# Rotary stage of a hybrid attention and state-space block: how the key norms are formed, and in what order four engines work

## The reference

```python
def rms_norm(u, g):
    uf = u.astype(F32)
    return (uf * lax.rsqrt(jnp.mean(uf * uf, -1, keepdims=True) + RMS_EPS) * g).astype(u.dtype)

def apply_axial_rope(u, cos, sin):
    ...
    out = jnp.stack([u1 * cs - u2 * sn, u1 * sn + u2 * cs], axis=-2)

out_a = window_sink_attention(apply_axial_rope(to_heads(aq), cos, sin), apply_axial_rope(to_heads(ak), cos, sin), ...)
cbk, cbv = rms_norm(to_heads(cbk), k_gain), to_heads(cbv)
out_b = global_block_attention(apply_axial_rope(rms_norm(to_heads(bq), q_gain), cos, sin),
                               apply_axial_rope(rms_norm(to_heads(bk), k_gain), cos, sin), ...)
```

## Time and profile before

| | us |
|---|---|
| median of three runs (lowest, highest) | 3442.82 (3438.43, 3443.50) |
| the profiled execution, its own time | 3442.47 |
| its span from first to last instruction | 3440.7 |
| the stage in layer 0, first instruction to attend's first product | 168.05 to 211.55 |
| the stage in layer 1 | 1999.22 to 2037.95 |

### The profile page before, as it was taken

How to read it: one execution, slowest core, us unless ns; L and a number is a source line. 1 busy time by engine, 2 the same in 40 slices (tenths; PEclk the granted TensorE clock), 3 DMA queues, 4 the chain that set the end, 5 groups by cost and what they waited for, 6 DMA issues and landing times. The chain is left out here.

```text
span 3440.7 us, 44530 instructions
## 1 busy us (share of the span) xinstructions
PE 3234.4 (94%) x17014; PEld 2739.6 (80%) x17014; DVE 1777.7 (52%) x2884; ACT 1009.9 (29%) x1949; POOL 1382.1 (40%) x1027
## 2 busy tenths in 40 slices
PE   5979989899999999999998979989899999999997
PEld 4768878788788888888886759878787788888886
DVE  8377958685673333333235867936776511311224
ACT  5257742361430000000003347732453300000003
POOL 0154213264444344343444354212354444454454
PEclk9979999999999999999999979999999999999999
DMA  8200023003111212111111610011022111111111
GB/s 332 74 1 1 1 101 107 21 25 123 59 52 62 67 67 68 66 61 61 43 37 66 228 38 1 1 50 50 13 86 80 49 55 49 43 55 49 43 55 50
DMA packets 69808, 214.12 MB, mean 62 GB/s; under 512 B 6816, under 2 KB 19104, under 8 KB 68256
## 3 DMA queue, kind: packets, MB, share of 16 engines
q1 hardware_dynamic: 62224, 183.86, 15.5%
q10 hardware_dynamic: 7440, 28.34, 2.3%
HBM read 192.78 MB, written 19.40 MB: 62 GB/s over the span
## 5 line engine op out<-in xcount | busy, mean ns | idle before, releaser
L205 PE MATMUL ps<-h_hi,f_whi 128*128 128x512 f32 (+1 forms) x1760 | 650.2, 369 | 3.5 <-DVE f_gated L3379 3.5
L206 PE MATMUL ps<-h_lo,f_whi 128*128 128x512 f32 (+1 forms) x1760 | 648.6, 369 | 0.0
L207 PE MATMUL ps<-h_hi,f_wlo 128*128 128x512 f32 (+1 forms) x1760 | 648.0, 368 | 0.0
L3379 DVE TENSOR_TENSOR f_gated<-f_gated,ps 128x512 f32<-128x512 f32 (+1 forms) x110 | 69.6, 634 | 812.6 <-PE ps L207 811.3
L3193 POOL TENSOR_TENSOR f_whi<-f_wraw,small 128x1024 fp32r<-128x1024 f32 x130 | 247.6, 1905 | 555.3 <-PE ps L207 529.7
L3390 DVE SCALAR_TENSOR_TENSOR x_res<-ps,mod,x_res 128x512 f32<-128x512 f32 (+1 forms) x448 | 308.3, 688 | 245.2 <-PE ps L207 244.4
L205 PEld LDWEIGHTS ps<-h_hi,f_whi 128*128 128x128 f32 x1760 | 332.3, 189 | 60.9 <-DVE f_gated L3379 3.9
L206 PEld LDWEIGHTS ps<-h_lo,f_whi 128*128 128x128 f32 x1760 | 332.1, 189 | 55.9 <-issue 1.0
L207 PEld LDWEIGHTS ps<-h_hi,f_wlo 128*128 128x128 f32 x1760 | 332.1, 189 | 55.4
L205 PE MATMUL ps<-f_ahi,f_whi 128*128 128x512 f32 (+1 forms) x896 | 337.4, 377 | 0.6 <-DVE x_res L3390 0.5
L3195 POOL TENSOR_TENSOR f_wlo<-f_wraw,f_whi 128x1024 fp32r<-128x1024 f32 x130 | 327.0, 2516 | 10.2
(11 more groups left out here) (321 smaller groups left out, 6450.7 us busy)
## 6 DMA issues: line engine op xcount, KB each, us to landing
f_wraw<-in_w_ffn SPq DMA_DIRECT2D x130, 512.0 KB, 3.2
ada_w<-in_w_ada SPq DMA_DIRECT2D x80, 512.0 KB, 5.2
later_w<-in_w_ada ACTq DMA_DIRECT2D x32, 512.0 KB, 3.2
o_wraw<-in_w_out SPq DMA_DIRECT2D x28, 512.0 KB, 3.3
wrawc<-in_w_in SPq DMA_DIRECT2D x26, 512.0 KB, 4.2
wrawab<-in_w_in SPq DMA_DIRECT2D x16, 512.0 KB, 6.6
x_res<-x_spill SPq DMA_DIRECT2D x6, 1024.0 KB, 8.1
x_res<-in_xT SPq DMA_DIRECT2D x8, 640.0 KB, 7.4
```

The source lines that it names most:

```text
L205: pe.matmul(out, w_hi, h_hi, start=first, stop=False)
L206: pe.matmul(out, w_hi, h_lo, start=False, stop=False)
L207: return pe.matmul(out, w_lo, h_hi, start=False, stop=last)
L3379: dve.tensor_tensor(g, g, pl.bank(3 + c, tn), ALU.mult).then_inc(u_taken[c], 1)
```

## The change

1. Key sums are made like the query sums: two-column products per 128 tokens (`sums`, now L865), so 10 tiles of tokens give a 128 x 20 result in bank 6. ScalarE takes one root of it (L805), VectorE one small reciprocal (L960), ScalarE copies it with each value repeated 64 times to `k_wide` (128 x 1280, L810), and PE turns that back to features on partitions with 10 products against the identity (`spread`, L871) into banks 0, 1 and 7. VectorE multiplies straight from PSUM (L931).
2. PE does four rotations before anything else; ScalarE begins with `bring(0)`. The squares of two query chunks come ahead of the keys'.
3. ScalarE does `bring(4)` between the two halves of the key copies.
4. `k_lo` moves from the end of VectorE's program to behind turn 3, ahead of the two turns of keys.
5. The staging reads `pl.qk` without the copy to `qst`; one half stays on GpSimd, the other becomes the last work of VectorE (`stage_half`, L773, L774, L776).

```diff
--- before.py
+++ after.py
...
-    squares = [(K, c) for c in ORDER] + q_parts
+    keys = [(K, c) for c in ORDER]
+    squares = [(3, 0), (3, 1)] + keys + [part for part in q_parts if part not in ((3, 0), (3, 1))]
+    keys_summed = 2 + len(keys)
...
-    rt = [pl.at(f"{tag}_rt{s}", [P, 512], F32, kb=173 + 2 * s) for s in range(2)]
-    ri = [pl.at(f"{tag}_ri{s}", [P, 512], F32, kb=177 + 2 * s) for s in range(2)]
+    k_root, k_inv = (pl.at(f"{tag}_k_{x}", [P, TT, 2], F32, kb=173 + 0.25 * n) for n, x in enumerate(("root", "inv")))
+    k_wide = pl.at(f"{tag}_k_wide", [P, TT, 2, HD], F32, kb=174)
...
+    spread_bank = {0: 0, 1: 1, 2: 7}
+    q_src = pl.qk[:, 2:4, :].rearrange("p k (t q) -> p k t q", q=P)
...
+    def stage_half(eng, p0):
+
+        h0 = 2 * (p0 // HD)
+        part = lambda z: z[p0:p0 + HD, h0:h0 + 2, :]
+        first = q_src[p0:p0 + HD, :, 0, :]
+        one = pl.small[p0:p0 + HD, 2:3].unsqueeze(2).broadcast_to([HD, 2, P])
+        eng.wait_ge(done[0], 6)
+        eng.tensor_tensor(part(att.q_two), first, one, ALU.mult).then_inc(q_hi_done[h0 // 2], 1)
+        eng.tensor_tensor(part(att.q_pad), first, one, ALU.mult).then_inc(q_padded, 1)
+        eng.wait_ge(q_hi_done[h0 // 2], 1)
+        eng.tensor_tensor(att.q_two[HD - p0:P - p0, h0:h0 + 2, :], first, raw(part(att.q_two)), ALU.subtract) \
+            .then_inc(q_padded, 1)
...
+            bring(0)
             square(0)
             square(1)
-            for n in range(NK):
-                tn = CHUNKS[squares[n][1]][1]
-                act.wait_ge(summed, n + 1)
-                if n >= 2:
-                    act.wait_ge(inverted, n - 1)
-                act.activation(rt[n % 2][:, 0:tn], pl.bank(n % 2, tn), ACT.Sqrt,
-                               bias=pl.small[:, 0:1]).then_inc(rooted, 1)
-                square(n + 2)
-                bring(n)
-            for n in range(NK + 2, N):
+            bring(1)
+            for n in range(2, keys_summed):
                 square(n)
-                if n - 2 < 5:
-                    bring(n - 2)
-            for m in range(N - 2, 5):
-                bring(m)
+            bring(2)
+            act.wait_ge(summed, keys_summed)
+            act.activation(k_root[:, :, :], pl.bank(6)[:, 64:64 + 2 * TT].rearrange("p (t h) -> p t h", h=2),
+                           ACT.Sqrt, bias=pl.small[:, 0:1]).then_inc(k_rooted, 1)
+            square(keys_summed)
+            bring(3)
+            act.wait_ge(k_inverted, 1)
+            act.activation(k_wide[:, :, :, :], k_inv[:, :, :].unsqueeze(3).broadcast_to([P, TT, 2, HD]),
+                           ACT.Copy).then_inc(k_widened, 1)
+            for n in range(keys_summed + 1, N):
...
+                if j == 0:
+                    bring(4)
             act.activation(k_round[:, :], pl.qk[:, 0, :], ACT.Copy).then_inc(k_copied, 1)
...
-            def key_sum(n):
-                tn = CHUNKS[squares[n][1]][1]
-                pe.wait_ge(squared, n + 1)
-                if n >= 2:
-                    pe.wait_ge(rooted, n - 1)
-                pe.matmul(pl.bank(n % 2, tn), pl.c(BLOCK64), sq[n % 2][:, 0:tn], start=True,
-                          stop=True).then_inc(summed, 1)
...
+            halves = pl.c(BLOCK64).rearrange("p (h d) -> p h d", h=2)[:, :, 0]
+
+            def sums(n):
...
-                halves = pl.c(BLOCK64).rearrange("p (h d) -> p h d", h=2)[:, :, 0]
                 for j in range(tn // P):
-                    first = (t0 // P + j) * HEADS
-                    out = pl.bank(6)[:, first:first + HEADS].rearrange("p (h k) -> p h k", k=2)[:, :, t - 3]
+                    tok = t0 // P + j
+                    if t == K:
+                        out = pl.bank(6)[:, 64 + 2 * tok:66 + 2 * tok]
+                    else:
+                        out = pl.bank(6)[:, tok * HEADS:(tok + 1) * HEADS].rearrange("p (h k) -> p h k", k=2)[:, :, t - 3]
                     mm = pe.matmul(out, sq[n % 2][:, j * P:(j + 1) * P], halves, start=True, stop=True)
                 mm.then_inc(summed, 1)
 
-            b = 0
-            for n in range(N):
-                if n < NK:
-                    key_sum(n)
-                else:
-                    query_sums(n)
-                if n < len(turns_a):
-                    rotate_a(n)
-                if n >= 1 and b < 4:
-                    rotate_b(b)
-                    b += 1
-            for m in range(N, len(turns_a)):
-                rotate_a(m)
-            for m in range(b, len(turns_b)):
-                rotate_b(m)
+            def spread(c):
+                t0, tn = CHUNKS[c]
+                for j in range(tn // P):
+                    mm = pe.matmul(pl.bank(spread_bank[c])[:, j * P:(j + 1) * P],
+                                   k_wide[:, t0 // P + j, :, :].rearrange("p h d -> p (h d)"), pl.c(IDENT),
+                                   start=True, stop=True)
+                mm.then_inc(k_spread, 1)
+
+            rotate_a(0)
+            rotate_a(1)
+            rotate_b(0)
+            rotate_b(1)
+            for n in range(keys_summed):
+                sums(n)
+            rotate_a(2)
+            sums(keys_summed)
+            rotate_a(3)
+            rotate_b(2)
+            for n in range(keys_summed + 1, N):
+                sums(n)
+            pe.wait_ge(k_widened, 1)
+            for _, c in keys:
+                spread(c)
+            rotate_a(4)
+            rotate_b(3)
+            rotate_a(5)
+            rotate_b(4)
+            rotate_b(5)
...
-            pool.wait_ge(normed, 2)
-            src = pl.qk[:, 2:4, :].rearrange("p k (t q) -> p k t q", q=P)
-            for n, p0 in enumerate((0, HD)):
-                h0 = 2 * n
-                part = lambda z: z[p0:p0 + HD, h0:h0 + 2, :]
-                if n == 1:
-                    pool.wait_ge(q_padded, 4)
-                pool.wait_ge(done[0], 6)
-                pool.tensor_copy(part(att.qst), src[p0:p0 + HD, :, 0, :]).then_inc(q_copied, 1)
-                pool.wait_ge(q_copied, n + 1)
-                one = pl.small[p0:p0 + HD, 2:3].unsqueeze(2).broadcast_to([HD, 2, P])
-                pool.tensor_tensor(part(att.q_two), part(att.qst), one, ALU.mult).then_inc(q_hi_done, 1)
-                pool.tensor_tensor(part(att.q_pad), part(att.qst), one, ALU.mult).then_inc(q_padded, 1)
-                pool.wait_ge(q_hi_done, n + 1)
-                pool.tensor_tensor(att.q_two[HD - p0:P - p0, h0:h0 + 2, :], part(att.qst),
-                                   raw(part(att.q_two)), ALU.subtract).then_inc(q_padded, 1)
+            stage_half(pool, 0)
...
             def key_norm(n):
-                t, c = squares[n]
+                t, c = keys[n]
                 t0, tn = CHUNKS[c]
-                dve.wait_ge(rooted, n + 1)
-                dve.reciprocal(ri[n % 2][:, 0:tn], rt[n % 2][:, 0:tn]).then_inc(inverted, 1)
-                dve.wait_ge(inverted, n + 1)
+                dve.wait_ge(k_spread, n + 1)
                 x = pl.qk[:, qk_slot(t), t0:t0 + tn]
-                dve.scalar_tensor_tensor(out=x, in0=x, scalar=gain_k, in1=ri[n % 2][:, 0:tn],
+                dve.scalar_tensor_tensor(out=x, in0=x, scalar=gain_k, in1=pl.bank(spread_bank[c], tn),
                                          op0=ALU.mult, op1=ALU.mult).then_inc(normed, 1)
...
-            key_norm(0)
-            key_norm(1)
             turn(0)
-            key_norm(2)
-            for m in range(1, 4):
-                turn(m)
+            dve.wait_ge(k_rooted, 1)
+            dve.reciprocal(k_inv[:, :, :], k_root[:, :, :]).then_inc(k_inverted, 1)
+            turn(1)
+            turn(2)
+            for n in range(NK):
+                key_norm(n)
+            turn(3)
+            dve.wait_ge(k_copied, 1)
+            dve.tensor_tensor(att.k_lo[:, 0, :], pl.qk[:, 0, :], raw(k_round[:, :]), ALU.subtract)
...
-            dve.wait_ge(k_copied, 1)
-            dve.tensor_tensor(att.k_lo[:, 0, :], pl.qk[:, 0, :], raw(k_round[:, :]), ALU.subtract)
+            dve.wait_ge(q_padded, 2)
+            stage_half(dve, HD)
```

More of the change, by code:

```diff
@@ L747, in norm_and_rotate @@
     inv_q = pl.at(f"{tag}_inv_q", [P, TT * HEADS], F32, kb=158.75)
-    squared, summed, rooted, inverted, normed = (pl.sem(f"{tag}_{x}") for x in
-                                                 ("squared", "summed", "rooted", "inverted", "normed"))
+    squared, summed, normed = (pl.sem(f"{tag}_{x}") for x in ("squared", "summed", "normed"))
+    k_rooted, k_inverted, k_widened, k_spread = (pl.sem(f"{tag}_{x}") for x in
+                                                 ("k_rooted", "k_inverted", "k_widened", "k_spread"))
     q_rooted, q_inverted, rot_ready = (pl.sem(f"{tag}_{x}") for x in
@@ L754, in norm_and_rotate @@
     brought = pl.sem(f"{tag}_brought")
-    q_padded, q_copied, q_hi_done, k_copied = (pl.sem(f"{tag}_{x}") for x in
-                                               ("q_padded", "q_copied", "q_hi_done", "k_copied"))
```

(2 more changed lines are left out.)

4 lines of the change are left out of this document (2 added, 2 removed).

## The result

| | before | after |
|---|---|---|
| median, 20 runs each (lowest, highest) | 3441.68 (3438.43, 3443.50) | 3449.44 (3443.50, 3452.63) |
| profiled execution: its time, its span | 3442.47, 3440.7 | 3447.53, 3445.7 |
| stage in layer 0: from, to, length | 168.05, 211.55, 43.50 | 168.65, 216.42, 47.77 |
| stage in layer 1 | 1999.22, 2037.95, 38.73 | 2001.54, 2044.10, 42.56 |

A forecast was written before the change was run, and what follows sets the result against it. It took the last engine at the barrier, GpSimd before the change, to set each stage's end. Layer 0 +2.6, layer 1 +6.2, less 2.8 for returning full clock, made +6.0 us: 3448.8, range 3435 to 3455.

The forecast's parts named there:

- main case: Both stages: half clock through PE's later sums, one chain through all engines, VectorE last; +6.0 us, chance 0.44.
- the give-back: PE's last spreads and rotation of A 4: full clock returns partway into the spreads, saving 1.4 us per layer.
- the clock is at half from 169.14 to 172.54 and I keep that: Layer 0's first four rotations on PE: half clock kept as before the change, so they end at 173.2.
- gains 0.6, turns 2.35 each: VectorE's tail behind k_round: two gains 0.6 us, both turns of keys 4.7 us, ahead of its staging.
- the port rule: Staging: VectorE with two SBUF inputs and GpSimd take a port pair in turns; if met, up to 1.9 us per layer.
- a change outside these two stages of more than 2 us: Rest of the kernel, outside both edited stages: a change of more than 2 us would show the prediction wrong.
- the held clock: Rival: PE stays at full clock through the sums in both stages; -7.8 us together, 3435.0, chance 0.24.
- GpSimd alone would end some 4 us sooner: Stage end, each layer: GpSimd's staging falls from eight steps to three, about 1.9 us; counts only if nothing ends later.

The follow-up runs named there:

- e4: Changed kernel with a one-column Sqrt as ScalarE's first instruction of the stage, so the table loads early; 3449.15 us, ratio 1.0018 to the kernel before.
- e11: Changed kernel with unread two-column products on PE, four in place of each wide filler of e5; 3464.25 us, ratio 1.0056 to the kernel before.
- e1: Kernel before with the new staging alone, one half on GpSimd and one last on VectorE; 3439.10 us, ratio 0.9992 to the kernel before.
- e12: Changed kernel with layer 0's two gains moved from behind k_lo to ahead of the key norms; 3446.05 us, ratio 1.0020 to the kernel before.
- e5: Changed kernel with unread 512-column products on PE, seven in layer 0 and six in layer 1; 3442.46 us, ratio 1.0007 to the kernel before.
- e6: Changed kernel with the old staging, eight steps, all on GpSimd; 3446.53 us, ratio 1.0018 to the kernel before.
- e3: Changed kernel with rotation of A 4 put ahead of the last sums and the spreads on PE; 3442.34 us, ratio 1.0001 to the kernel before.
- e8: Changed kernel with three moves: k_lo behind the scales, rotation of A 4 ahead of later sums and spreads, table load first; 3437.79 us, ratio 0.9993 to before.
- e9: e8 with the wide fillers of e5 added; 3437.56 us, ratio 0.9986 to the kernel before.
- e7: Changed kernel reordered: key squares, sums and root first, query sums between rotations, k_lo behind the scales; 3439.61 us, ratio 0.9996 to the kernel before.

## Why the prediction was right, and where it was off

The forecast was 3448.8 with 3435 to 3455, the result is 3449.44. The main case held: half clock through the sums, one chain to `k_round`, VectorE last. Steps of layer 0, counted from the stage's own start:

| step | forecast | measured |
|---|---|---|
| four rotations end | 5.1 | 6.2 |
| root of the keys | 15.3 | 16.4 |
| widening | 20.5 | 21.5 |
| later sums end | 25.2 | 26.2 |
| rotation of A 4 usable | 31.5 (less 1.4) | 31.0 |
| `k_round` | 35.9 (less 1.4) | 35.4 |
| VectorE ends | 45.1 (less 1.4) | 46.4 |
| attend | 44.7 (the 1.4 is off) | 47.8 |

- **Right**: every wait of the chain and its order; the price of the spread at half (0.43 a tile, ten in 4.3; e4 4.51, e11 4.61) and at full (0.24 a tile; 2.48 in layer 1); the widening at 1.26; the give-back in layer 0, about 1.5 for 1.4. The views named to decide it read as said: GpSimd idle 4.03 and 6.92 us before turns 2 and 4, ScalarE 4.98 before `bring(4)`, VectorE's `k_lo` released by `k_round`.
- **Off, start**: "the clock is at half from 169.14 to 172.54 and I keep that". Half was there from the first product, at 168.69, and lasted to about 174: the rotations ended 1.1 us later, and the chain with them.
- **Off, VectorE's tail**: gains 0.6, turns 2.35 each. Measured in layer 0: gains 2.68, turns 4.79 together, as priced; in layer 1, which has no gains, the turns 6.3 where I had 4.7. From `k_round` to attend it is 2.3 and 1.8 us longer than priced (the barrier, 1.35 for 0.9, is 0.45 of it in layer 0, `k_lo`, 1.79 for 1.48, is 0.3 in each; in layer 0 the scales were 0.6 cheaper). I had named the port rule (the Trainium skill, SBUF — State Buffer, section "SBUF: two separate sides") for the staging, where the halves did not meet, and not for the key turns and gains, which run beside GpSimd's last steps. The same page, section "Who interferes with whom", counts `tensor_scalar` among what can take the shared pair, and the trace agrees: 2.68 for two beside GpSimd, against 0.61 in the profile before (two of 0.35 that overlap), where GpSimd waited. e1 and e12 show the same cost on other instructions.
- **Off, layer 1**: "1.4 per layer". The clock was back at full by 2024.71, before the spreads, not in the middle of them; `bring(4)` came 2.8 us earlier than forecast. So layer 1 lost 3.8 instead of 4.8, layer 0 4.3 instead of 1.2: the sum, 8.1 for 6.0, is nearer than its parts. That the median came within 0.7 us of 3448.8 is luck: the stages were 2.1 us over, in parts of opposite sign, and the rest of the execution came out shorter.
- **A sign of being wrong that showed**: "a change outside these two stages of more than 2 us". In the profiled pair it is 3.1 us. The medians do not bear it out (7.8 in all against 8.1 in the stages), and the stretch between the stages varies by more than that among kernels that do not differ there (1783.90 to 1790.55); as a sign it was drawn too narrow.
- **The rivals**: the held clock did not come by itself; e5 shows what it is worth, 7.0 us of the medians against my 13.8 (its own fillers, up to 6 us a layer, are in that).
- **The gain**: "GpSimd alone would end some 4 us sooner". In layer 0 it ended at 211.28, as long after the stage's start as before, because it waited for `bring(4)`, and its three steps took 2.84 us (208.44 to 211.28), not 1.9. The split staging saves where GpSimd ends last: 2.5 us in e1, against some 0.5 in the changed order (e6).

What stays open: how much of e3 is order and how much a clock that the new order brings; what the fillers add to the three moves (e8, e9); whether e7 is faster than the kernel before; and what moves the clock's rise, and with it an unchanged stretch by up to 3.2 us, from one execution to the next.

## What to carry to other kernels

Busy is not enough to have the full clock: here two-column products kept TensorE busy for 16.00 of 16 us at 0.50 (e11), while the same sums with wide products between them ran at 1.00 for 20 us (e5). So try narrow products between wide ones that are due anyway, as in e3, and look at the granted clock of the stretch. Before a step is made shorter, ask which engine will end next and what stands behind its first wait: here a chain through four engines took the end from the engine that was relieved. And price every VectorE instruction beside a working GpSimd by rows taken beside a working GpSimd.
